# Bias with row maximum, and multiplicities with row sum, as one VectorE instruction per query tile in a ten-phase transformer kernel

## The chip, the cores and the metric

The kernel runs on one core of one Trainium2 chip. The metric is the device time of one execution in microseconds (us); three executions of the kernel before took 1783.36, 1783.44 and 1785.34 us, median 1783.44. Less is better. Shorter names used below: PE is TensorE, DVE is VectorE, ACT is ScalarE, POOL is GpSimd.

## The reference, cut to what matters

A residual stream of 256 tokens by 1024 channels, float32, passes through ten phases: two layers with a three-part mixer and a feed-forward, then two layers of feed-forward, mixer, feed-forward. Three of the attentions matter here. The differential attention of the first two mixers:

```python
dist = jnp.abs(qp[:, None] - pos[None, :]).astype(jnp.float32)
bias = -slopes[:, None, None] * dist
s1 = jnp.einsum('bqhd,bkhd->bhqk', q1b, k1).astype(jnp.float32) * scale + bias
s2 = jnp.einsum('bqhd,bkhd->bhqk', q2b, k2).astype(jnp.float32) * scale + bias
p = jax.nn.softmax(s1, axis=-1) - lam * jax.nn.softmax(s2, axis=-1)
```

It has 4 heads of width 48, each with two score matrices, and its queries and keys are RMS-normed with a gain. The banded attention of the "even" mixer (8 heads, a mask, a sink per head) is `softmax(where(valid, s, NEG_INF))` with the sink in maximum and sum. The "odd" mixer joins three dilated branches by their maxima and sums, which equals one softmax in which each key counts as many times as branches see it:

```python
wts = jnp.stack(ls) * jnp.exp(ms - jnp.max(ms, axis=0))
att = jnp.einsum('rbsh,rbshd->bshd', wts, jnp.stack(outs).astype(jnp.float32))
att = (att / jnp.sum(wts, axis=0)[..., None]).astype(h.dtype)
```

## The kernel before, in words

Every engine has its own instruction list, written out by hand, and they meet at counting semaphores. `PHASES` gives the order: mix1 0, ffn1 0, mix1 1, ffn1 1, ffn2 0, even, ffn2 1, ffn2 2, odd, ffn2 3.

All large products stream 128-column units of weights. SP loads a unit into a ring of 4 (`raw`), ACT makes its high part (`wh`, L525), DVE its low part (`wl`, L804), PE multiplies (L1210 to L1212 for the input projections of the mixers, L1223 to L1227 elsewhere). The instruction that splits unit i+4 stands in DVE's list behind the one that takes unit i out of PSUM (`y`, L1095).

In a mixer the table `W` says behind which unit of the input projection each further step stands, in the same order for every engine. Step `("attn", t)` does at once: on PE the transposition of the probabilities of head t-3 (L1327), the scores of head t (L1316) and the output of head t-4 (L1344 or L1351); on DVE `row_max` of head t and `normalise` of head t-1; on ACT the copy of the transposed probabilities (L597) and the exponentials of head t (L567). One "row" r is one 256x256 score matrix: 128 partitions by 2 query tiles of 256 keys, so 512 elements a partition. A plain head has one row, a differential head has two.

`row_max` (from L952) on a head with a bias writes `tab * bias + scores` to `pr` (L963), takes the maximum per query tile (L966) and scales it (L971). The 6 plain heads of a mix1 phase have no bias and take the maximum from PSUM. `normalise` (from L973) for the odd mixer multiplies the exponentials with the multiplicities (L981) and sums them (L982); elsewhere the sum comes out of ACT's exponential. Then come the reciprocal (L985) and the scaling (L998, or L987 to L995 for differential heads). The helper `link` puts a wait for the instruction just issued behind it: DVE goes on only when it is complete. An instruction without `link` lets the next one follow at once.

In the differential heads `tab` holds the distance |q-k| and `bias` is minus the slope times the square root of 48; in the even and odd mixers `tab` holds the mask and `bias` is 1. `head_norm` (L862) applies gain and inverse root to queries and keys. `start_values` (from L823) runs once, behind unit 8 of the first mixer, and makes small constants.

Step `post` (mix1) and `ln` (even) close a mixer, then PE starts the output projection, whose operand `mx` needs all heads.

Of the kernel before, what the change touches and what calls it, by code (L numbers as in the profile page):

```python
# [13 lines left out]
SEQ = 256  # L14
# [2 lines left out]
KD = FC // 2  # L17
RING = 4
EPS = 1e-6


PHASES = [("mix1", 0), ("ffn1", 0), ("mix1", 1), ("ffn1", 1), ("ffn2", 0), ("even", 0),
# [76 lines left out]
def build_program(nc, xin, wa, wb, prm_d, row_d, const_d, bias_d, mask_d, pw_d, out):  # L99
# [21 lines left out]
    with ctx:  # L121
        def sb(name, shape, dt=f32, c=ctx):
            return c.enter_context(nc.sbuf_tensor(name, shape, dt))
# [15 lines left out]
        tab = sb("tab", [P, 1024])  # L139
# [8 lines left out]
        eps = sb("eps", [P, 1])  # L148
        par = sb("par", [P, 32])
        small = sb("small", [P, 96])  # L150

        with ExitStack() as turn:
            gux = sb("gux", [P, 2, FC * SEQ], r32, turn)
# [29 lines left out]
        def yc(c, n=1):  # L183
            return y[:, c * SEQ:(c + n) * SEQ]
# [12 lines left out]
        def col(name, n=0):  # L197
            return prm[:, PRM[name] + n:PRM[name] + n + 1]
# [587 lines left out]
        def _(dve):  # L786
# [37 lines left out]
            def start_values():  # L824

                dve.wait_ge(s_prm, 16)
                dve.wait_ge(s_con, 48)
                dve.wait_ge(s_one, 16)
                nc.vector.tensor_copy(msk[:, :, :].rearrange("p a b -> p (a b)"), prf[:, 0:NL * P])
                l0, l1 = prm[:, PRM["lb"]:PRM["lb"] + 2], prm[:, PRM["lb"] + 2:PRM["lb"] + 4]  # L830
                link(nc.vector.tensor_tensor(par[:, 16:18], l0, l1, ALU.max))
                nc.vector.tensor_tensor(par[:, 0:2], l0, par[:, 16:18], ALU.subtract)
                nc.vector.tensor_tensor(par[:, 2:4], l1, par[:, 16:18], ALU.subtract)
                prod = qqf[:, 0:192].rearrange("p (a b) -> p a b", a=4)
                link(nc.vector.tensor_tensor(prod, view(row[:, 0:1], [[96, 4], [1, 48]]),
                                             view(row[:, 48:49], [[96, 4], [1, 48]]), ALU.mult))
                nc.vector.reduce_sum(par[:, 4:8], prod, axis=AX.X).then_inc(s_ini, 1)
                dve.wait_ge(s_inie, 1)
                link(nc.vector.tensor_tensor(par[:, 16:18], par[:, 8:10], par[:, 10:12], ALU.add))
                link(nc.vector.reciprocal(par[:, 18:20], par[:, 16:18]))  # L840
                nc.vector.tensor_tensor(par[:, 0:2], par[:, 8:10], par[:, 18:20], ALU.mult)
                link(nc.vector.tensor_tensor(par[:, 2:4], par[:, 10:12], par[:, 18:20], ALU.mult))

                link(nc.vector.tensor_tensor(par[:, 4:6], par[:, 0:2], par[:, 2:4], ALU.add))
                link(nc.vector.tensor_tensor(par[:, 20:22], par[:, 0:2], par[:, 0:2], ALU.subtract))
                link(nc.vector.tensor_tensor(par[:, 22:24], par[:, 4:6], par[:, 0:2], ALU.subtract))
                link(nc.vector.tensor_scalar(par[:, 20:24], par[:, 20:24], 0.0, None, ALU.max))
                link(nc.vector.tensor_scalar(par[:, 24:28], par[:, 20:24], -1.0, 1.0, ALU.mult, ALU.add))
                for l in range(2):
                    lam0 = 0.8 - 0.6 * math.exp(-0.3 * l)  # L850
                    link(nc.vector.tensor_tensor(par[:, 28 + l:29 + l], par[:, 13 + 2 * l:14 + 2 * l],
                                                 par[:, 12 + 2 * l:13 + 2 * l], ALU.subtract))
                    link(nc.vector.tensor_scalar(par[:, 28 + l:29 + l], par[:, 28 + l:29 + l], lam0, None, ALU.subtract))
# [4 lines left out]
            def head_norm(m, g, kind, l):  # L858
                c, gains, _ = qk_groups(kind, l)[g]
                dve.wait_ge(m["qk_rsd"], g + 1)  # L860
                for k, (name, at0) in enumerate(gains):
                    ins = nc.vector.scalar_tensor_tensor(out=yc(c + k), in0=yc(c + k), scalar=col(name, at0),  # L862
                                                         in1=sq[:, k * SEQ:(k + 1) * SEQ], op0=ALU.mult, op1=ALU.mult)
                ins.then_inc(m["qk_normed"], 1)

# [87 lines left out]
            def row_max(m, hs, t):  # L953
                h = hs[t]
                for k in range(len(h.rows)):
# [4 lines left out]
                    if h.bias is not None:  # L960
                        if r >= 6:
                            dve.wait_ge(m["probs_turned"], row_owner(hs, r - 6) + 1)
                        link(nc.vector.scalar_tensor_tensor(out=pr[:, r % 6, :], in0=tab[:, 0:512], scalar=h.bias,  # L963
                                                            in1=s, op0=ALU.mult, op1=ALU.add))
                        s = pr[:, r % 6, :]
                    link(nc.vector.reduce_max(small[:, 16 + o:18 + o], pair(s), axis=AX.X))  # L966
                    if h.sink is not None:
                        link(nc.vector.tensor_scalar(small[:, 16 + o:18 + o], small[:, 16 + o:18 + o], scale,
                                                     row[:, ROW_SINK + h.sink:ROW_SINK + h.sink + 1], ALU.mult, ALU.max))
# [3 lines left out]
            def normalise(m, hs, t, l):  # L973
# [4 lines left out]
                dve.wait_ge(m["exps"], r + nr)  # L978
                if h.cnt is not None:

                    link(nc.vector.tensor_tensor(pr[:, r % 6, :], pr[:, r % 6, :], tab[:, 512:1024], ALU.mult))  # L981
                    link(nc.vector.reduce_sum(sums, pair(pr[:, r % 6, :]), axis=AX.X))  # L982
                if h.sink is not None:
                    link(nc.vector.tensor_tensor(sums, sums, small[:, 24 + o:26 + o], ALU.add))
                link(nc.vector.reciprocal(small[:, 80 + o:80 + o + 2 * nr], sums))  # L985
# [620 lines left out]
```

## Time and profile before

| what | value |
|---|---|
| median of 3 runs | 1783.44 us |
| the profiled execution's own time | 1782.92 us |
| its span in the trace | 1781.1 us |
| PE busy | 1680.6 us (94%) |
| DVE busy | 1243.1 us (70%), 1956 instructions |
| ACT busy | 944.6 us (53%) |
| POOL busy | 512.1 us (29%) |

Span and own time differ by 1.8 us. A timeline row gives start, duration and engine, then line, operation, written tile <- read tiles, shapes and how many instructions it joins; in square brackets stands how long the engine had been idle before it and who ended that. On DVE a duration may overlap the next instruction by some 0.08 us, so the cost of an instruction in a queue is the distance between two starts.

### The profile page before, as it was taken

The numbers are of one execution on the slowest core, as the hardware profiler recorded it, in microseconds if no ns is written. First come the engines' busy times: TensorE is split into PE (matmuls) and PEld (weight loads), VectorE is DVE, ScalarE is ACT, GpSimd is POOL, SyncE is SP. The second block draws the span as 40 slices with busy tenths as digits, with TensorE's granted clock in tenths as the row PEclk, the third lists the DMA queues.
The fourth block names the chain that finished last, engine by engine and source line by source line (L and its number), as shares of the span: only waits on it lengthen the run. The fifth ranks groups of instructions, "written<-read, shape, count | busy, mean of one in ns | idle before, by whom it ended". The sixth has DMA issues, their size and how long they took to land. (4 is left out here: it accounts for less than half of the span.)

```text
span 1781.1 us, 30420 instructions
## 1 busy us (share of the span) xinstructions
PE 1680.6 (94%) x10326; PEld 1464.6 (82%) x10326; DVE 1243.1 (70%) x1956; ACT 944.6 (53%) x1550; POOL 512.1 (29%) x492
## 2 busy tenths in 40 slices
PE   7896999999987999999999978999999999799999
PEld 6784899988866999888888847888888889578887
DVE  5776777757786777667766867776577766867764
ACT  5444566544553666466646545665466534356652
POOL 0040433310213334134420004443144311444430
PEclk9998999999998999999999989999999999899999
DMA  6330355644312556555654303656465654236563
GB/s 248 106 108 24 120 188 183 219 162 152 106 59 71 166 188 203 187 172 183 208 197 132 117 1 119 187 188 209 159 188 187 209 181 154 72 108 191 186 216 101
DMA packets 71065, 274.13 MB, mean 154 GB/s; under 512 B 7888, under 2 KB 9040, under 8 KB 70992
## 3 DMA queue, kind: packets, MB, share of 16 engines
q1 hardware_dynamic: 70992, 273.17, 47.5%
q8 instruction: 44, 0.72, 0.2%
q14 instruction: 29, 0.24, 0.0%
HBM read 272.09 MB, written 1.05 MB: 153 GB/s over the span
## 5 line engine op out<-in xcount | busy, mean ns | idle before, releaser
L804 DVE TENSOR_TENSOR wl<-raw,wh 128x1024 fp32r<-128x1024 f32 (+1 forms) x474 | 624.3, 1317 | 127.6 <-ACT wh L525 121.1
L525 ACT ACTIVATE wh<-raw 128x1024 fp32r<-128x1024 f32 (+1 forms) x474 | 529.9, 1118 | 228.3 <-PE gb L1227 126.5
L1223 PE MATMUL gb<-hx,wh 128*128 128x512 f32 x1540 | 553.6, 398 | 0.0
L1224 PE MATMUL gb<-hx,wl 128*128 128x256 f32 x1540 | 432.2, 281 | 0.0
L1223 PE MATMUL gb<-gux,wh 128*128 128x512 f32 x960 | 341.3, 394 | 0.0
L1223 PEld LDWEIGHTS gb<-hx,wh 128*128 128x128 f32 x1540 | 289.8, 188 | 60.5
L1210 PE MATMUL gb<-hx,wh 128*128 128x256 f32 x1008 | 299.9, 298 | 17.7 <-DVE hx L821 9.6
L1224 PEld LDWEIGHTS gb<-hx,wl 128*128 128x128 f32 x1540 | 291.0, 189 | 7.9
L1211 PE MATMUL gb<-hx,wh 128*128 128x256 f32 x1008 | 288.9, 287 | 0.0
L1212 PE MATMUL gb<-hx,wl 128*128 128x256 f32 x1008 | 288.5, 286 | 0.0
L1224 PE MATMUL gb<-gux,wl 128*128 128x256 f32 x960 | 268.2, 279 | 0.0
L511 POOL TENSOR_TENSOR tap<-tap,rstd 128x256 f32<-128x256 f32 x132 | 175.5, 1329 | 246.0 <-ACT tap L724 139.3
L1210 PEld LDWEIGHTS gb<-hx,wh 128*128 128x128 f32 x1008 | 196.0, 194 | 30.2 <-issue 18.3
L1223 PEld LDWEIGHTS gb<-gux,wh 128*128 128x128 f32 x960 | 180.0, 188 | 39.0
L1211 PEld LDWEIGHTS gb<-hx,wh 128*128 128x128 f32 x1008 | 196.5, 195 | 5.2 <-issue 2.7
L514 POOL TENSOR_TENSOR gux<-gu,gux 128x256 f32 x132 | 142.9, 1083 | 198.9 <-ACT gux L733 198.9
L1212 PEld LDWEIGHTS gb<-hx,wl 128*128 128x128 f32 x1008 | 196.2, 195 | 0.0
L1224 PEld LDWEIGHTS gb<-gux,wl 128*128 128x128 f32 x960 | 180.4, 188 | 4.3
L430 POOL TENSOR_TENSOR sq<-x 128x256 f32<-128x256 f32 x63 | 65.0, 1031 | 241.8 <-DVE x L1170 223.2
L542 ACT ACTIVATE hx<-x,prm 128x256 fp32r<-128x256 f32 (+1 forms) x80 | 40.1, 508 | 147.1 <-DVE x L1170 143.0
L1223 PE MATMUL gb<-mx,wh 128*128 128x512 f32 x224 | 86.0, 420 | 11.4 <-DVE mx L951 7.8
L730 ACT ACTIVATE ptb<-gb 128x256 f32<-128x256 f32 x132 | 50.1, 379 | 85.0 <-PE gb L1227 85.0
(211 smaller groups left out, 2074.9 us busy)
## 6 DMA issues: line engine op xcount, KB each, us to landing
raw<-in_wa SPq DMA_DIRECT2D x378, 512.0 KB, 3.5
raw<-in_wb SPq DMA_DIRECT2D x96, 704.0 KB, 4.2
x<-in_x SPq DMA_DIRECT2D x2, 512.0 KB, 6.2
out_x<-x SPq DMA_DIRECT2D x8, 128.0 KB, 3.0
row<-in_row SPq DMA_DIRECT2D x1, 836.0 KB, 11.1
tab<-in_bias SPq DMA_DIRECT2D x3, 256.0 KB, 4.5
con<-in_const SPq DMA_DIRECT2D x1, 544.0 KB, 9.1
tab<-in_bias SPq DMA_DIRECT2D x1, 512.0 KB, 5.4
```

What stands on the lines that cost most here:

```text
L430: link(nc.gpsimd.tensor_tensor(sq[:, 0:SEQ], xc, xc, ALU.mult))
L511: nc.gpsimd.tensor_tensor(tap[:, j, :], tap[:, j, :], rstd[:, :], ALU.mult).then_inc(s_up, 1)
L514: nc.gpsimd.tensor_tensor(gul[:, part], gu[:, j, :], guh[:, part].bitcast(f32), ALU.subtract).then_inc(s_gul, 1)
L525: nc.scalar.activation(wh[:, slot, 0:nt * P], raw[:, slot, 0:nt * P], ACT.Copy).then_inc(s_hi, 1)
L542: nc.scalar.activation(hh[:, part], x[:, part], ACT.Copy, scale=prm[:, at0]).then_inc(s_hh, 1)
L730: nc.scalar.activation(low[:, j, 1, :], gb[2 * j + 1][:, SEQ:2 * SEQ], ACT.Copy).then_inc(s_vl, 1)
L804: nc.vector.tensor_tensor(wl[:, slot, 0:nt * P], raw[:, slot, 0:nt * P], wh[:, slot, 0:nt * P].bitcast(f32), ALU.subtract).then_inc(s_lo, 1)
L1210: nc.tensor.matmul(bank, a, rhs_h(k), start=start and k == 0, stop=False)
L1211: nc.tensor.matmul(bank, a, rhs_l(k), start=False, stop=False)
L1212: last = nc.tensor.matmul(bank, b, rhs_h(k), start=False, stop=stop and k == nt - 1)
L1223: nc.tensor.matmul(bank[:, :], a, both(k), start=start and k == 0, stop=False)
L1224: nc.tensor.matmul(bank[:, 0:SEQ], b, high(k), start=False, stop=False)
```

## The change

`row_max` on a head with a bias issues one `tensor_tensor_reduce` per query tile in place of L963 and L966: `pr = (tab + scores) * bias`, with the maximum of that row as a second result. `normalise` in the odd mixer issues one per query tile in place of L981 and L982. Only the second of each two is followed by `link`. For `(tab + s) * bias` to be the old `tab * bias + s`, the queries of the differential heads are divided by `bias`, through eight more gain columns `bqs` that `start_values` computes.

```diff
+LOWEST = -3.0e38
...
+        bqs = small[:, 88:96]
...
                 for l in range(2):
+                    for h in heads("mix1"):
+                        if h.bias is not None:
+                            nc.vector.tensor_scalar(bqs[:, 4 * l + h.h:4 * l + h.h + 1], col("bq", l), 1.0 / h.bias, None, ALU.mult)
...
-                    ins = nc.vector.scalar_tensor_tensor(out=yc(c + k), in0=yc(c + k), scalar=col(name, at0),
+                    gain = col(name, at0) if name != "bq" else bqs[:, 4 * l + (c - M1_B) // 2:4 * l + (c - M1_B) // 2 + 1]
+                    ins = nc.vector.scalar_tensor_tensor(out=yc(c + k), in0=yc(c + k), scalar=gain,
                                                          in1=sq[:, k * SEQ:(k + 1) * SEQ], op0=ALU.mult, op1=ALU.mult)
...
-                        link(nc.vector.scalar_tensor_tensor(out=pr[:, r % 6, :], in0=tab[:, 0:512], scalar=h.bias,
-                                                            in1=s, op0=ALU.mult, op1=ALU.add))
-                        s = pr[:, r % 6, :]
-                    link(nc.vector.reduce_max(small[:, 16 + o:18 + o], pair(s), axis=AX.X))
+                        for qt in range(2):
+                            cs = slice(qt * SEQ, (qt + 1) * SEQ)
+                            last = nc.vector.tensor_tensor_reduce(out=pr[:, r % 6, cs], in0=tab[:, cs], in1=s[:, cs], scale=h.bias,
+                                                                  scalar=LOWEST, op0=ALU.add, op1=ALU.max,
+                                                                  accum_out=small[:, 16 + o + qt:17 + o + qt])
+                        link(last)
+                    else:
+                        link(nc.vector.reduce_max(small[:, 16 + o:18 + o], pair(s), axis=AX.X))
...
-                    link(nc.vector.tensor_tensor(pr[:, r % 6, :], pr[:, r % 6, :], tab[:, 512:1024], ALU.mult))
-                    link(nc.vector.reduce_sum(sums, pair(pr[:, r % 6, :]), axis=AX.X))
+                    for qt in range(2):
+                        p1 = pr[:, r % 6, qt * SEQ:(qt + 1) * SEQ]
+                        last = nc.vector.tensor_tensor_reduce(out=p1, in0=p1, in1=tab[:, 512 + qt * SEQ:512 + (qt + 1) * SEQ], scale=1.0,
+                                                              scalar=0.0, op0=ALU.mult, op1=ALU.add,
+                                                              accum_out=sums[:, qt:qt + 1])
+                    link(last)
```

The lists of PE, ACT, POOL and SP stay as they were. On DVE, one head of the odd mixer before (`row_max` of a head, `normalise` of the head before it, then the next unit):

```order
L963 SCALAR_TENSOR_TENSOR pr<-tab,mb 128x512
L966 TENSOR_REDUCE small<-pr 128x2
L971 TENSOR_SCALAR small<-small 128x2
L981 TENSOR_TENSOR pr<-pr,tab 128x512
L982 TENSOR_REDUCE small<-pr 128x2
L985 RECIPROCAL small<-small 128x2
L998 TENSOR_SCALAR pr<-pr,small 128x256 x2
L1095 TENSOR_TENSOR y<-gb,rstd 128x256
L804 TENSOR_TENSOR wl<-raw,wh 128x1024
```

The same place in the changed kernel, whose line numbers are shifted (L981, L999, L1012, L1109 and L806 are the old L971, L985, L998, L1095 and L804):

```order
L971 ISA pr,small<-tab,mb 128x256
L971 ISA small 128x1
L971 ISA pr,small<-tab,mb 128x256
L971 ISA small 128x1
L981 TENSOR_SCALAR small<-small 128x2
L993 ISA pr,small<-pr,tab 128x256
L993 ISA small 128x1
L993 ISA pr,small<-pr,tab 128x256
L993 ISA small 128x1
L999 RECIPROCAL small<-small 128x2
L1012 TENSOR_SCALAR pr<-pr,small 128x256 x2
L1109 TENSOR_TENSOR y<-gb,rstd 128x256
```

Each `tensor_tensor_reduce` is two instructions: the work on 256 elements, and one that writes the reduced value of one element. Two instructions have become four in each of the 32 biased rows and 8 multiplicity rows. The second place is `start_values` on DVE, in the changed kernel:

```order
L849 TENSOR_SCALAR par<-par 128x4
L850 TENSOR_SCALAR par<-par 128x4
L854 TENSOR_SCALAR small<-prm 128x1 x4
L856 TENSOR_TENSOR par<-par 128x1
L858 TENSOR_SCALAR par<-par 128x1
L854 TENSOR_SCALAR small<-prm 128x1 x4
L856 TENSOR_TENSOR par<-par 128x1
```

The two groups of four at L854 are new; nothing is linked to them.

## Rows read from the trace of the kernel before

**Rows 1.** The page: busy us (share of the span) x instructions of each engine.
```profile
PE 1680.6 (94%) x10326; PEld 1464.6 (82%) x10326; DVE 1243.1 (70%) x1956; ACT 944.6 (53%) x1550; POOL 512.1 (29%) x492
```

**Rows 2.** Groups of DVE instructions by form: count, busy us, mean ns, idle before.
```profile
L963 DVE SCALAR_TENSOR_TENSOR pr<-tab,mb 128x512 f32<-128x512 f32 x32 | 21.9, 685 | 8.7 <-PE mb L1316 8.7
L981 DVE TENSOR_TENSOR pr<-pr,tab 128x512 f32<-128x512 f32 x8 | 6.0, 754 | 0.0
L995 DVE SCALAR_TENSOR_TENSOR pr<-pr,small 128x256 f32<-128x256 f32 x16 | 7.0, 481 | 0.3
```

**Rows 3.** Timeline of DVE, one head of the odd mixer.
```profile
1509.92 0.17 DVE L971 TENSOR_SCALAR small<-small 128x2 f32<-128x2 f32 x1
1510.00 0.68 DVE L981 TENSOR_TENSOR pr<-pr,tab 128x512 f32<-128x512 f32 x1
...
1511.44 0.17 DVE L985 RECIPROCAL small<-small 128x2 f32<-128x2 f32 x1
1511.64 0.62 DVE L998 TENSOR_SCALAR pr<-pr,small 128x256 f32<-128x256 f32 x2
1512.17 0.42 DVE L1095 TENSOR_TENSOR y<-gb,rstd 128x256 f32<-128x256 f32 x1
1512.51 1.22 DVE L804 TENSOR_TENSOR wl<-raw,wh 128x1024 fp32r<-128x1024 f32 x1
```

**Rows 4.** Timeline of ACT, even mixer: exponentials that also give a row sum.
```profile
1042.87 0.51 ACT L567 ACTIVATE pr<-pr,small 128x256 f32<-128x256 f32 x1 [2.37 <-DVE small L971]
1043.28 0.19 ACT L567 ACTIVATION_READ_ACCUMULATOR pr<-pr,small 128x1 f32 x1
1043.38 0.49 ACT L567 ACTIVATE pr<-pr,small 128x256 f32<-128x256 f32 x1
```

**Rows 5.** Timeline of DVE, two 512-element instructions with no wait between.
```profile
39.84 0.68 DVE L871 TENSOR_TENSOR ptb<-mb,con 128x512 f32<-128x512 f32 x1
40.44 0.68 DVE L872 TENSOR_TENSOR y<-y,con 128x512 f32<-128x512 f32 x1
```

**Rows 6.** Timelines at the end of mixer mix1 0, DVE and PE.
```profile
148.79 0.88 DVE L862 SCALAR_TENSOR_TENSOR y<-y,prm,sq 128x256 f32<-128x256 f32 x2 [1.65 <-ACT sq L620]
...
160.46 1.78 PE L1344 MATMUL mb<-tv,ptb 128*128 128x96 f32 x7 [4.58 <-DVE mx L1029]
```

**Rows 7.** Timeline of PE, even mixer: two waits.
```profile
1025.01 0.48 PE L1360 MATMUL mb<-sq,con 128*128 128x256 f32 x1 [2.03 <-POOL sq L444]
...
1052.24 0.40 PE L1351 MATMUL mb<-ptb,tv 128*64 128x256 f32 x1 [2.59 <-ACT ptb L597]
```

**Rows 8.** The chain that ended last, in order of time: start us, us, what.
```profile
1018.77 0.61 DVE pr L963
...
1047.94 0.70 DVE pr L963
...
1503.90 0.61 DVE pr L963
...
1550.14 0.60 DVE pr L981
```

**Rows 9.** Timeline of PE, odd mixer: three waits.
```profile
1523.79 0.63 PE L1327 MATMUL mb<-con,pr 128*128 128x128 f32 x4 [2.05 <-ACT sq L618]
...
1546.47 0.63 PE L1327 MATMUL mb<-con,pr 128*128 128x128 f32 x4 [1.84 <-DVE mx L1086]
...
1553.98 1.09 PE L1327 MATMUL mb<-con,pr 128*128 128x128 f32 x4 [3.24 <-DVE mx L1086]
```

**Rows 10.** Windows of odd: PE, PEld, DVE, ACT, POOL busy, granted clock, DMA share, GB/s.
```profile
1519.00:1525.00 6.00, 2.57 (x10) 1.33 (x10) 5.83 (x12) 3.60 (x6) 2.82 (x4) 0.98 0.27 87
1525.00:1534.00 9.00, 9.00 (x39) 6.67 (x37) 5.29 (x12) 2.21 (x5) 3.03 (x7) 0.64 0.17 58
```

**Rows 11.** Timelines of DVE and PE, mix1 0, behind unit 8.
```profile
60.04 1.23 DVE L804 TENSOR_TENSOR wl<-raw,wh 128x1024 fp32r<-128x1024 f32 x1 [1.71 <-ACT wh L525]
...
85.20 0.58 PE L1210 MATMUL gb<-hx,wh 128*128 128x256 f32 x1 [5.09 <-DVE y L1095]
```

## The prediction

> **What bounds the kernel now.** First the page: PE is busy for 94% of the span and DVE for 70% [rows 1], so a faster DVE helps only where PE stands idle for it. Such places are the ends of the mixers and most of the odd mixer, so I read the waits of PE there, then DVE's timeline in the same stretches, then the chain that ended last. The chain covers the part from 1001 us on; for the two mix1 phases I followed the timelines.
>
> What the change touches are pairs of two 512-element instructions, each followed by a wait for its completion: L963 with L966 (32 times), L981 with L982 (8 times, 754 ns in the mean against 685, because single ones run beside POOL) [rows 2]. In the queue a pair takes from 1510.00 to 1511.44, that is 1.44 us [rows 3].
>
> **The new pair.** It is work on 256 elements, read-out, work on 256 elements, read-out, and a wait only behind the last. No row shows such an instruction, so I price it by its nearest neighbours. Two-input work on 256 elements, with no wait behind it, holds the queue from 1512.17 to 1512.51, 0.34 us. A tiny instruction without a wait holds it from 1509.92 to 1510.00, 0.08 us, and one with a wait from 1511.44 to 1511.64, 0.20 us [rows 3]. The sum is 0.34 + 0.08 + 0.34 + 0.20 = 0.96 us, a saving of 0.48 us a pair. That is the low end, too: no piece has a cheaper neighbour. That the parts overlap like this is what ACT does with its own row sums: the read-out is recorded at 0.19 us but holds the queue for 0.10 (1043.28 to 1043.38), and the main instruction before it holds it for 0.41 of its 0.51 [rows 4]. The high end: the reduction takes two cycles an element, so each half costs what 512 elements cost, and every part runs to its end before the next starts: twice (0.72 + 0.20) = 1.84 us, with half of today's 1.44 for one of 512 elements, 0.40 dearer than today. I take 0.96, since rows 3 and rows 4 both show the queue moving on before an instruction ends.
>
> **Which pairs lie on the path.** A pair counts where DVE's end is what PE finally waits for.
>
> - mix1, twice: the heads of the differential attention are DVE's at the very end. In mix1 0 DVE last waits for ACT at 148.79; from there it works without a pause through the rows of the last two heads, 4 pairs, to the instruction for which PE waits 4.58 us at 160.46 [rows 6]. The pairs of the first two such heads are hidden: PE's last projection unit and the products of the scan (L1394) cover them. With that cover gone they would still be behind POOL's squares. mix1 1 repeats the pattern. So 2 x 4 pairs, 8 x 0.48 = 3.8 us.
> - even: 8 pairs, of which the chain holds 3, from 1018.77 to 1047.94 [rows 8]. The first ends in PE's wait for POOL at 1025.01 (2.03 us); the others, one head before the last but one and the last, end in PE's waits up to the one of 2.59 us at 1052.24 [rows 7]. Between the first and the second PE's convolution products bound, and pairs vanish beneath them. 3 x 0.48 = 1.4 us.
> - odd: 16 pairs, 12 in the chain, from L963 at 1503.90 to L981 at 1550.14 [rows 8]. Six come before PE's wait of 2.05 us at 1523.79, four before the 1.84 us at 1546.47, two before the 3.24 us at 1553.98 [rows 9]. The first six ask for 2.9 us, more than that wait; but PE stood idle for 6 - 2.57 = 3.4 us between 1519 and 1525 [rows 10], the rest of it for POOL's squares, which follow a late L1095 of DVE. So there is room. 12 x 0.48 = 5.8 us.
>
> Together 23 pairs, 11.0 us. What is late next is PE itself, or ACT in the heads' exponentials, which move with the maxima.
>
> **What it adds.** Eight tiny instructions in `start_values`, 8 x 0.08 = 0.64 us. They look hidden in 1780 us and are not: they stand ahead of unit 8's L1095 and of a row maximum; ACT's exponentials and with them its next weight split follow that maximum, DVE waits for the split (1.71 us at 60.04), and this goes round until PE waits 5.09 us for DVE at 85.20 [rows 11]. So +0.6 us. The gain column of `head_norm` only comes from another tile, same form: nothing. The longer exposure of `small` costs nothing.
>
> **The clock.** In the odd mixer PE was busy for only 2.57 us of the 6 us from 1519 to 1525, and then worked through 9 us at a granted clock of 0.64, at 1.2 instead of 2.4 GHz for most of it [rows 10]. In that stretch PE is the bound, so the low clock costs (1 - 0.64) x 9 = 3.2 us. The change takes 2.9 us out of just this idle time. If most of the gap closes, the clock need not fall, and 3.2 us come back; DVE's own work there (two more pairs, shorter by 1 us) would just keep up. I count it in. Elsewhere the idle gaps of PE stay long (4.58 us at 160.46 becomes 2.7) and I take the clock as unchanged, plus or minus 1.5 us.
>
> **Sum.** -11.0 + 0.6 - 3.2 = -13.6 us against the profiled execution's 1782.92 us: 1769.3. The median of the runs stands 0.5 us above it, so I forecast 1769.8 us. A measurement of this kernel can tell about 0.2%, 3.6 us, from no change.
>
> **A rule that speaks against it.** The 16 instructions at L995, a scalar-tensor-tensor with both inputs in SBUF, took 481 ns for 256 elements [rows 2], and L1095 with one input in PSUM 0.42 us [rows 3]: two SBUF streams alone don't halve the rate here, which would be near the 685 ns of 512 elements. But neither has a reduced output. The Trainium skill, Vector Engine (DVE) Microarchitecture Reference, section "Points that are easy to get wrong", warns that a scalar-tensor-tensor with two SBUF sources that are not bf16 runs at half throughput, since no read port is left for the accumulator. By that rule the multiplicity pairs (both inputs in SBUF) would be slow and the bias pairs (scores in PSUM) not. No run here shows it.
>
> **The rivals.**
>
> 1. As forecast, but the clock falls all the same: 1769.8 + 3.2 = 1773.0 us. For it: other gaps of PE remain and a fall needs no large one; against it: the gap was 60% of six microseconds and is now nearly filled. Chance 0.27.
> 2. Reduction from two SBUF streams at half rate (the mechanism of the rule above). 512 elements with no wait hold the queue for 0.60 us [rows 5], so such a pair is 0.60 + 0.08 + 0.60 + 0.20 = 1.48 us, 0.52 more than forecast. Five of the 12 in the odd chain are of this kind: 2.6 us back, which also lets the gap at 1523 stand, 3.2 more at worst: 1772.4 to 1775.6. Chance 0.10.
> 3. Each read-out waits for the end of its main instruction, and the next for it: 0.45 + 0.20 + 0.45 + 0.20 = 1.30 us, with the 0.42 us of L1095 and the 0.03 us between the end of L985 and the next start [rows 3]. The saving is 0.14 x 23 = 3.2 us, less 0.6, and the clock stays low: 1783.4 - 2.6 = 1780.8 us, no change that can be told. Against it: rows 4. Chance 0.08.
> 4. The other side: two cycles an element in every reducing instruction, and no overlap, so 1.84 us a pair. 23 x 0.40 + 0.6 = 9.8 us: 1793.2 us. It decides from a pair of 1.41 us on (slower by more than 0.2% from 1.57). For it: four instructions replace two, of a kind that this program never ran. Against: ACT's reducing form is no slower than its plain one. Chance 0.05.
>
> The forecast has 0.45; 0.05 is left for what I don't see, such as the new instructions meeting POOL's as L981 did in its mean of 754 ns [rows 2].
>
> **Range and chances.** From 1765.5 (the clock also holds in one mixer's end) to 1777.5, which takes in rivals 1 and 2. Left out are rivals 3 and 4 and tails, under 0.2. Faster by over 0.2% (below 1779.9): forecast, rivals 1 and 2 and part of the rest, 0.86. Within 0.2%: rival 3, 0.08. Slower: 0.06.
>
> **What would show it.** In the new profile the two mains of a pair start 0.42 us apart, and the pair takes 0.96 us to the next start (rival 3: 1.30; rivals 2 and 4: 0.68 or more between the starts). PE's wait at the end of mix1 0 falls from 4.58 to about 2.7 us; the stretch from mix1's unit 8 to PE's wait at 85.20 is 0.6 us longer; the odd mixer from its first L963 to the output projection is 9 us shorter, with a granted clock near 1 where rows 10 have 0.64. Wrong would be a pair over 1.3 us, or a pair at 0.96 with the odd mixer shorter by less than 4 us.

## The result and the profile after

The changed kernel takes 1764.47 us (median of 4 runs, 1763.29 to 1764.66), the kernel before, on the same chip, 1783.4 us (4 runs, 1779.64 to 1785.34). The ratio is 0.9897, with an interval from 0.9882 to 0.9913. So the gain is 18.9 us, where 13.6 were forecast: the direction was right, and the time lies 1 us below the low end of the range, 1765.5.

| | before | after |
|---|---|---|
| median, us | 1783.4 | 1764.47 |
| span of the profiled execution, us | 1781.1 | 1762.7 |
| mean granted clock of TensorE | 0.971 | 0.978 |
| DVE busy, us | 1243.1 | 1221.2 |
| PE's wait at the end of mix1 0, us | 4.58 | 3.33 |
| PE's waits in odd, us: first / second / third | 2.05 / 1.84 / 3.24 | 1.02 / 0 / 4.32 |

The page of after, the line of busy times (before: [rows 1]):

```profile
PE 1669.1 (95%) x10326; PEld 1459.4 (83%) x10326; DVE 1221.2 (69%) x2044; ACT 943.8 (54%) x1550; POOL 511.0 (29%) x492
```

DVE has 88 instructions more and 22 us less busy time. PE is busy 11.5 us less for the same 10326 matmuls. The kernel has not taken work from PE, so those 11.5 us already point at the clock.

The groups of DVE's instructions after, by form: count, busy us, mean ns, idle before (before: [rows 2]):

```profile
L971 DVE CUSTOM_DVE_ANT_0 pr<-tab,mb 128x256 f32<-128x256 f32 x64 | 24.3, 416 | 9.9 <-PE mb L1330 9.9
L993 DVE CUSTOM_DVE_ANT_0 pr<-pr,tab 128x256 f32<-128x256 f32 x16 | 7.9, 531 | 0.0
L971 DVE DVE_READ_ACCUMULATOR2_ANT small<- 128x1 f32 x64 | 5.2, 82 | 0.0
L993 DVE DVE_READ_ACCUMULATOR2_ANT small<- 128x1 f32 x16 | 1.2, 77 | 0.0
```

And the timeline of DVE after, in one head of the odd mixer (before: [rows 3]):

```profile
1499.48 0.41 DVE L971 CUSTOM_DVE_ANT_0 pr<-tab,mb 128x256 f32<-128x256 f32 x1
1499.82 0.08 DVE L971 DVE_READ_ACCUMULATOR2_ANT small<- 128x1 f32 x1
1499.82 0.41 DVE L971 CUSTOM_DVE_ANT_0 pr<-tab,mb 128x256 f32<-128x256 f32 x1
1500.16 0.08 DVE L971 DVE_READ_ACCUMULATOR2_ANT small<- 128x1 f32 x1
1500.27 0.17 DVE L981 TENSOR_SCALAR small<-small 128x2 f32<-128x2 f32 x1
1500.35 0.42 DVE L993 CUSTOM_DVE_ANT_0 pr<-pr,tab 128x256 f32<-128x256 f32 x1
1500.69 0.08 DVE L993 DVE_READ_ACCUMULATOR2_ANT small<- 128x1 f32 x1
1500.69 0.42 DVE L993 CUSTOM_DVE_ANT_0 pr<-pr,tab 128x256 f32<-128x256 f32 x1
1501.04 0.08 DVE L993 DVE_READ_ACCUMULATOR2_ANT small<- 128x1 f32 x1
1501.15 0.17 DVE L999 RECIPROCAL small<-small 128x2 f32<-128x2 f32 x1
```

The reader is to compare the starts, not the durations. From 1499.48 to 1500.27 the pair holds the queue for 0.79 us: 0.34 + 0.34 + 0.11. A read-out starts at the same moment as the next main instruction, at 1499.82, so it takes no room of its own; and the wait behind the last one costs 0.11 us. The prediction had 0.96, with 0.08 and 0.20 for these two. The saving is 1.44 - 0.79 = 0.65 us a pair instead of 0.48.

**Where the time went.** PE issues the same matmuls in the same order in every kernel of this study, so its k-th matmul is the same work in all of them, and the difference of its starts is a running account. The table takes six marks, the matmuls that start nearest to 130, 200, 600, 1000, 1100 and 1480 us of before, and 1600 us as the last, and gives by how many us each stretch between them is shorter (-) or longer (+) than in the profile of before. The 400 us from 600 to 1000, the 380 us from 1100 to 1480 and all that follows 1600 move by 0.2 us at most in any kernel, and stand together as "rest".

| kernel | start, to 130 | end of mix1 0, to 200 | ffn and mix1 1, to 600 | even, 1000 to 1100 | odd, 1480 to 1600 | rest | span |
|---|---|---|---|---|---|---|---|
| forecast | +0.6 | -1.9 | -1.9 | -1.4 | -9.0 | 0 | -13.6 |
| the change | -0.31 | -3.56 | -1.03 | -3.83 | -9.66 | +0.03 | -18.37 |

The chain of reasons is in PE's waits. The timeline of PE after, at the end of mix1 0 (before: the wait of 4.58 us at 160.46, [rows 6]):

```profile
157.67 1.10 PE L1358 MATMUL mb<-tv,ptb 128*128 128x96 f32 x8 [3.33 <-DVE mx L1043]
```

The same for the even mixer (before: [rows 7]):

```profile
1019.47 0.70 PE L1374 MATMUL mb<-sq,con 128*128 128x256 f32 x2 [1.40 <-POOL sq L446]
1037.39 1.05 PE L1365 MATMUL mb<-ptb,tv 128*64 128x256 f32 x4 [0.99 <-DVE mx L1043]
1043.78 1.05 PE L1365 MATMUL mb<-ptb,tv 128*64 128x256 f32 x4 [2.10 <-ACT ptb L599]
1047.44 1.39 PE L1365 MATMUL mb<-ptb,tv 128*64 128x256 f32 x8 [0.44 <-DVE mx L1043]
```

And for the odd mixer (before: 1523.79, 1546.47 and 1553.98, [rows 9]):

```profile
1512.43 0.63 PE L1341 MATMUL mb<-con,pr 128*128 128x128 f32 x4 [1.02 <-ACT sq L620]
...
1529.70 0.63 PE L1341 MATMUL mb<-con,pr 128*128 128x128 f32 x4
...
1537.35 0.67 PE L1341 MATMUL mb<-con,pr 128*128 128x128 f32 x4 [4.32 <-DVE mx L1100]
```

In odd the first wait is halved, the second is gone, and the third has grown from 3.24 to 4.32 us, since PE now comes to it earlier. The windows of odd after, with the columns of [rows 10] (window, its length, busy us of PE, PEld, DVE, ACT and POOL, granted clock, DMA share, GB/s):

```profile
1508.00:1514.00 6.00, 4.98 (x32) 3.68 (x30) 5.44 (x17) 3.77 (x6) 3.89 (x7) 1.00 0.28 90
1514.00:1520.00 6.00, 6.00 (x39) 4.78 (x39) 3.83 (x15) 2.45 (x4) 2.41 (x5) 1.00 0.26 85
1520.00:1526.00 6.00, 6.00 (x40) 4.63 (x38) 5.84 (x16) 2.72 (x5) 3.97 (x5) 1.00 0.27 87
```

Where PE had stood idle for 3.4 of 6 us it is now idle for 1.0, and behind it the granted clock is 1.00, 2.4 GHz, where it had been 0.64 for nine microseconds.

### The profile page after: what moved, and what is told of

Read it like the earlier page. It is cut to its first block and busy times, and to the rows that moved or that the text cites. A ratio compares the mean times of both kernels' runs of the same rounds, so it can differ in the third digit from the quotient of the medians.

```text
span 1762.7 us, 30508 instructions
## 1 busy us (share of the span) xinstructions
PE 1669.1 (95%) x10326; PEld 1459.4 (83%) x10326; DVE 1221.2 (69%) x2044; ACT 943.8 (54%) x1550; POOL 511.0 (29%) x492
## 3 DMA queue, kind: packets, MB, share of 16 engines
HBM read 272.09 MB, written 1.05 MB: 155 GB/s over the span
## 5 line engine op out<-in xcount | busy, mean ns | idle before, releaser
L806 DVE TENSOR_TENSOR wl<-raw,wh 128x1024 fp32r<-128x1024 f32 (+1 forms) x474 | 624.7, 1318 | 129.0 <-ACT wh L527 122.8
```

The lines of the kernel that those rows point to most:

```text
L806: nc.vector.tensor_tensor(wl[:, slot, 0:nt * P], raw[:, slot, 0:nt * P], wh[:, slot, 0:nt * P].bitcast(f32), ALU.subtract).then_inc(s_lo, 1)
```

## The experiments

Twelve runs follow, of eleven kernels: the kernel with a wait behind both instructions ran twice, and one of the eleven is the change itself, again. Every time stands against runs of the kernel before on the same chip; the phase stretches are each profile's own. First the two halves of the change.

### Bias pairs alone

```diff
-                    for qt in range(2):
-                        p1 = pr[:, r % 6, qt * SEQ:(qt + 1) * SEQ]
-                        last = nc.vector.tensor_tensor_reduce(out=p1, in0=p1, in1=tab[:, 512 + qt * SEQ:512 + (qt + 1) * SEQ], scale=1.0,
...
-                    link(last)
+                    link(nc.vector.tensor_tensor(pr[:, r % 6, :], pr[:, r % 6, :], tab[:, 512:1024], ALU.mult))
+                    link(nc.vector.reduce_sum(sums, pair(pr[:, r % 6, :]), axis=AX.X))
```

> Only the bias pairs are fused (32 rows); the multiplicity pairs of the odd mixer stay as two 512-element instructions. 18 of the 23 path pairs are of this kind. Theory A (a fused pair costs 0.79 us, the read-outs take no room of their own, each saves 0.65): 18 x 0.65 - 0.6 = 11.1 us under the kernel before, 1772.3; and if the 2.6 us that the first four pairs of the odd mixer take from PE's idle time are enough to keep the clock up there, another 3.2 less: 1769.1. Theory B (a fused pair saves the forecast 0.48 and the rest of the gain came from the clock alone): 8.0 us without the clock, 1775.4.

Measured: 1764.63 us (1763.46 to 1766.16) against 1781.07, ratio 0.991 [0.9894, 0.9927], so 16.4 us. The even mixer is 3.91 us shorter, as with the whole change, and the odd one 8.98 of the 9.66. The bias pairs carry nearly all of the gain. Theory A had 14.3 us with the high clock, theory B 8.0; the result is above both and nearest to A.

### Multiplicity pairs alone

The edit is the other half: the bias pairs and the query gains as before, no work added in `start_values`.

> Only the 8 multiplicity pairs are fused; bias and maximum, the query gains and start_values are those of before. Five path pairs, two of them ahead of the idle time at 1523. Theory A: 5 x 0.65 = 3.3 us, and the clock still falls in the odd mixer because 2 us of idle time remain: 1780.2. If the clock holds all the same: 1777.0. The rule of half rate for two float32 inputs from SBUF with a reduction: no gain, 1783.4 or a little over.

Measured: 1777.3 us (1776.1 to 1779.76, 10 runs) against 1781.07, ratio 0.9981 [0.9971, 0.999], so 3.8 us, near theory A's 3.3. All eight pairs are in the odd mixer, which is 2.80 us shorter and runs 17.1 us at the half clock where before runs 20.5. DVE's timeline of this kernel, whose L983 is the fused instruction with both inputs in SBUF:

```profile
1506.54 0.42 DVE L983 CUSTOM_DVE_ANT_0 pr<-pr,tab 128x256 f32<-128x256 f32 x1
1506.88 0.08 DVE L983 DVE_READ_ACCUMULATOR2_ANT small<- 128x1 f32 x1
1506.88 0.42 DVE L983 CUSTOM_DVE_ANT_0 pr<-pr,tab 128x256 f32<-128x256 f32 x1
```

It takes 0.42 us and 0.34 of the queue, as L971 of after does with one input in PSUM. Rival 2 is refuted for this instruction. The Trainium skill, Vector Engine (DVE) Microarchitecture Reference, section "Points that are easy to get wrong", has a scalar-tensor-tensor with two SBUF sources that are not bf16 at half throughput; this fused multiplication and row sum, in float32 from two SBUF tiles, doesn't run so.

In the odd mixer the two halves give 8.98 + 2.80 = 11.8 us apart and 9.66 together. Part of it is the gap, which can be closed only once: the matmul at 1523.79 us of before comes 2.21 us earlier with the bias pairs, 0.87 with the multiplicity pairs and 2.68 with both. That is 0.4 of the 2.1 us. The rest arises behind it, and no run takes it apart. It is not time at the half clock counted twice: the halves remove 13.7 and 3.4 us of that, and the whole change removes 17.1.

### A wait behind both instructions of each pair

```diff
-                        link(last)
+                            link(last)
```

The `link`, a wait for completion, moves into the loop over the two query tiles; the same at the multiplicities. This kernel ran twice. The first time:

> The changed kernel with a wait for completion behind both instructions of a pair instead of behind the second alone. Theory A (the first read-out is hidden under the second main instruction): each half costs 0.45 us, a pair 0.90 instead of 0.79, 23 x 0.11 = 2.5 us more than the changed kernel, 1767.0. Rival (the read-out is free however it stands, the time is the main instruction's alone): under 1 us more.

Measured: 1764.35 us (1763.31 to 1765.9), ratio 0.9906 [0.9889, 0.9922]. DVE's timeline of this run:

```profile
1499.92 0.41 DVE L971 CUSTOM_DVE_ANT_0 pr<-tab,mb 128x256 f32<-128x256 f32 x1
1500.26 0.08 DVE L971 DVE_READ_ACCUMULATOR2_ANT small<- 128x1 f32 x1
1500.37 0.42 DVE L971 CUSTOM_DVE_ANT_0 pr<-tab,mb 128x256 f32<-128x256 f32 x1
1500.71 0.08 DVE L971 DVE_READ_ACCUMULATOR2_ANT small<- 128x1 f32 x1
1500.83 0.17 DVE L981 TENSOR_SCALAR small<-small 128x2 f32<-128x2 f32 x1
```

The pair takes 0.91 us, 0.12 more: 0.45 us to the next start behind each main instruction. The second time it stood beside the whole change (below):

> The whole change with a wait for completion behind both instructions of every pair, beside the whole change on the same chip. The trace of the first such run showed a pair of 0.91 us against 0.79. Theory A (a pair on the path costs what its queue room costs): 23 x 0.12 = 2.8 us over the whole change, less what the multiplicity pairs beside PE-bound stretches hide, so 1.5 to 2.8. Theory B (the first such run came out level with the whole change on another chip, so the wait is absorbed: PE, not DVE, bounds by now): under 0.7 us over it.

Measured: 1764.92 us (1762.17 to 1766.54, 5 runs) against the whole change's 1762.68; ratios to before 0.9905 [0.9889, 0.9922] and 0.9892 [0.9877, 0.9908]. The 2.2 us between the medians lie within theory A's 1.5 to 2.8, but the intervals overlap, so the times don't decide. PE's account shows which pairs count. At the end of mix1 0, where four pairs are on the path, PE's mark is 0.48 us later than in the changed kernel's profile (4 x 0.12), and as much at the end of mix1 1. In even, the three pairs make it later by 0.14, 0.26 and 0.39 us, one by one. In odd the marks at 1523.79, 1546.47 and 1553.98 us of before move by 0.03 us at most. So 8 + 3 pairs still set those marks, and the twelve in odd, once they are fused, do not.

The end of the program hardly feels even the eleven. In even the 0.39 us are gone at the mark of 1100 us. From the mark at 130 us to the end, the changed kernel's two profiles take 1632.9 and 1633.2 us, and the two of this kernel 1633.6 and 1632.9. By the marks theory A is right, by the total theory B. What gives the time back behind the marks is not taken apart here.

### The idle time of the odd mixer put back

```diff
             def attention(m, kind, hs, t, l):
+                if kind == "odd" and t == 3:
+                    for _ in range(4):
+                        link(nc.vector.tensor_tensor(gu[:, :, :], gu[:, :, :], gu[:, :, :], ALU.max))
                 if t < len(hs):
                     row_max(m, hs, t)
```

The four instructions leave their tile as it is. They were to take 2.9 us of DVE and take 3.7, since the first of them, which runs beside POOL, takes 1.53 us and the others 0.69:

```profile
1506.55 3.71 DVE L1037 TENSOR_TENSOR gu<-gu 128x512 f32<-128x512 f32 x4
1510.29 0.42 DVE L971 CUSTOM_DVE_ANT_0 pr<-tab,mb 128x256 f32<-128x256 f32 x1
```

> The changed kernel with four linked 512-element VectorE instructions on an unused buffer (0.72 us each, 2.9 us) ahead of the row maximum of head 3 in the odd mixer, which gives TensorE its idle time near the end of that head's step back. Theory of the clock: the granted clock falls to 1.2 GHz again for some 6 us behind it, as it did before, and the time rises by 2.9 + 3.2 = 6.1 us over the changed kernel, to 1770.6. Rival (the fall has nothing to do with this idle time): 2.9 us, 1767.4, and no stretch at half the clock there.

Measured: 1771.17 us (1769.92 to 1772.04), ratio 0.9946 [0.9929, 0.9963], 6.5 and 6.8 us above the two kernels that ran beside it with the bias pairs and without such idle time (1764.63 and 1764.35). The windows of odd:

```profile
1508.00:1514.00 6.00, 1.66 (x9) 0.86 (x8) 5.70 (x18) 2.67 (x5) 0.81 (x3) 0.85 0.20 77
1514.00:1520.00 6.00, 6.00 (x17) 3.69 (x18) 4.09 (x15) 1.90 (x4) 2.89 (x5) 0.50 0.27 87
1520.00:1526.00 6.00, 6.00 (x34) 4.90 (x32) 1.73 (x2) 1.54 (x2) 1.80 (x3) 0.80 0.00 0
```

With PE busy for only 1.66 of 6 us, the next six run at 0.50, at 1.2 GHz, on 17 matmuls where the whole change has 39. By PE's account the instructions make it 3.3 us later at once, and the low clock 3.9 us more by 1540 us of before. By the end of the mixer it is 7.3 us behind the changed kernel. That is the prediction's mechanism, in its direction and its size: idle time at this place costs about twice what it lasts.

### The whole change again, and the gains on POOL

> The whole change again, unchanged, as the measure for the three kernels that run beside it. 1764.5 us, as before, if the chip is like the others; the sum of the two part gains measured apart (16.4 for the bias pairs with the start values, 3.8 for the multiplicity pairs) would be 20.2 us. Theory A (the parts partly buy the same thing, the high clock of the odd mixer, which either needs only once, and from the first six pairs of the odd mixer PE becomes the bound): the whole gains 0.5 to 3 us less than that sum, 17.2 to 19.7. Theory B (the parts are independent): 20.2 us, within 0.5.

Measured: 1762.68 us (1762.22 to 1764.76, 5 runs) against 1781.7 (15 runs), ratio 0.9892 [0.9877, 0.9908], so 19.0 us against 20.2 for the halves. That is within A, but the intervals are too wide to separate A from B by the times; the odd mixer's stretches above do.

```diff
+            pool.wait_ge(s_prm, 16)
+            for l in range(2):
+                for h in heads("mix1"):
+                    if h.bias is not None:
+                        last = nc.gpsimd.tensor_scalar(bqs[:, 4 * l + h.h:4 * l + h.h + 1], col("bq", l), 1.0 / h.bias, None, ALU.mult)
+            link(last)
```

(ahead of POOL's first phase, and gone from `start_values`).

> The whole change, but the eight tiny inverse-slope gains are computed by POOL before its first phase instead of by DVE in start_values. Theory A (they stand on DVE's path at the start and cost 0.47 us there, as the marks of PE show by 68.8 us): 0.4 to 0.6 us under the whole change of the same chip, PE's mark at 68.8 us earlier by that, and no other difference. Theory B (they are hidden, and the 0.47 us came from something else): no difference. Rival on the other side: POOL's own first work shifts by the eight instructions, at most 1 us later, and PE waits for it: same or up to 0.5 us slower.

Measured: 1764.32 us (1760.37 to 1764.83, 5 runs), ratio 0.9901 [0.9886, 0.9917]: no difference that the times can tell from the whole change. PE's account between 55 and 89 us of before shows one: in the whole change, and also in the kernel with mix1 alone, the matmul at 68.77 us loses 0.48 us against before; with the gains on POOL it loses 0.00, and so it does in the kernel without gains (odd alone, below). So the added work costs 0.48 us where the prediction had 0.6, and it sits where the prediction put it. Taking it away is right in the profile and too small to be confirmed in the time; I don't call this version faster.

### One mixer at a time

Three kernels fuse the pairs in one kind of mixer and leave the others as before. Mix1 alone keeps the query gains and their start values; odd alone and even alone have neither. The edit of the kernel before, for odd (the multiplicities in the same way):

```diff
-                        link(nc.vector.scalar_tensor_tensor(out=pr[:, r % 6, :], in0=tab[:, 0:512], scalar=h.bias,
-                                                            in1=s, op0=ALU.mult, op1=ALU.add))
-                        s = pr[:, r % 6, :]
-                    link(nc.vector.reduce_max(small[:, 16 + o:18 + o], pair(s), axis=AX.X))
+                        if kind == "odd":
+                            for qt in range(2):
...
+                            link(last)
+                        else:
+                            link(nc.vector.scalar_tensor_tensor(out=pr[:, r % 6, :], in0=tab[:, 0:512], scalar=h.bias,
+                                                                in1=s, op0=ALU.mult, op1=ALU.add))
+                            link(nc.vector.reduce_max(small[:, 16 + o:18 + o], pair(pr[:, r % 6, :]), axis=AX.X))
```

> Fused bias pairs in the two mix1 phases alone; even, odd and the multiplicities as before the change, the start values kept. Theory A (8 pairs on the path at 0.65 us each, 0.5 us of start values, clock unchanged but for 0.5 to 1 us at the end of mix1 0): 4.7 to 5.7 us under before, so about 1776. Theory B (pairs worth the 0.48 us of the prediction, no clock): 3.3 us. Theory C (the 3 us by which the clock outran the forecast comes from mix1's ends): 7.5 us or more. In the trace the half-clock stretch of the odd mixer must be there again, about 6.8 us long.

> Both kinds of pair fused in the odd mixer alone, everything else as before the change (no start values). Theory A (the odd mixer gives 5.1 us by its pairs and 4.6 by the clock, and neither depends on the other phases): 9 to 10.5 us under before, the stretch at 1525 to 1534 us at the high clock and the mixer's last stretch shorter at the low clock. Theory B (the high clock in the odd mixer needs the state that the earlier phases leave): 5 to 6.5 us, the half-clock stretch stands. Theory C (the pairs are worth more here than the marks of PE say): over 11 us.

> Bias pairs fused in the even mixer alone. Theory A (3 pairs on the path and some clock at the mixer's end): 2.0 us by the pairs and 0 to 2 us by the clock, so 2 to 4 us under before. Theory B (the prediction's sizes): 1.4 us and no clock. Theory C (the clock of the even mixer's end goes the other way round without the changed phases ahead): 0 to 1 us, or slower. With the mix1 phases alone (3.1 us measured, 4.7 to 5.7 expected) and the odd mixer alone the three sum to the whole's 19 us if the phases are independent: 3.1 + 9.7 + 3 is 15.8, so one of them should then be larger than A says.

Measured: mix1 alone 1778.58 us (10 runs), ratio 0.9984 [0.9974, 0.9994], 3.1 us, nearest theory B's 3.3; odd alone 1772.38 us (4 runs), ratio 0.9948 [0.9932, 0.9965], 8.4 us by the medians, a little under A's 9 to 10.5; even alone 1780.07 us (10 runs), ratio 0.9998 [0.9988, 1.0007], nothing that can be told, theory C. For mix1 alone B has the number but not the reason: its profile has the four pairs at the end of mix1 0 at 2.48 us, 0.62 each, as the whole change has, and loses time elsewhere (below). The three ratios leave 0.70% together (0.16 + 0.02 + 0.52), the whole change has 1.08%. So the parts don't add up: 0.38% are missing, about 7 us, more than the four intervals together explain if their errors are independent (0.27%). The stretches of the profiles say where, and how many us PE ran at the half clock in even and odd (worked out as twice the stretch times one minus its mean granted clock):

| kernel | start | end of mix1 0 | to 600 | even | odd | half clock in even | half clock in odd |
|---|---|---|---|---|---|---|---|
| before | 0 | 0 | 0 | 0 | 0 | 20.5 | 20.5 |
| the change | -0.31 | -3.56 | -1.03 | -3.83 | -9.66 | 17.1 | 3.4 |
| the change, again | -0.34 | -3.39 | -0.92 | -3.97 | -9.66 | 17.1 | 3.4 |
| bias pairs alone | -1.67 | -3.77 | -1.14 | -3.91 | -8.98 | 17.1 | 6.8 |
| multiplicity pairs alone | -2.26 | -0.14 | -0.44 | -0.66 | -2.80 | 20.5 | 17.1 |
| idle time put back | -2.28 | -2.55 | -1.83 | -3.87 | -2.37 | 17.1 | 13.7 |
| a wait behind both, first | -0.33 | -3.21 | -0.96 | -3.82 | -9.50 | 17.1 | 3.4 |
| a wait behind both, second | -2.64 | -3.39 | -1.31 | -3.84 | -9.61 | 17.1 | 3.4 |
| gains on POOL | -3.47 | -3.93 | -1.85 | -3.83 | -9.61 | 17.1 | 3.4 |
| mix1 alone | -2.70 | -3.74 | -1.16 | -0.49 | +0.98 | 20.5 | 20.5 |
| odd alone | -2.53 | +0.15 | -0.05 | 0.00 | -7.38 | 20.5 | 10.2 |
| even alone | -2.38 | -0.04 | -0.02 | -1.00 | +0.95 | 23.9 | 20.5 |

Three things are to be seen. First, a stretch in which nothing was fused stays as it was within 0.7 us, but for odd, which is 1 us longer in two kernels that leave it alone. With it mix1 alone adds up roughly: -3.74 - 1.16 in its own stretches, -0.49 in even, +0.98 in odd and +0.5 for the gains are -3.9, where the medians have 3.1 us. Second, even and odd gain more in the whole change than when fused alone, 3.83 against 1.00 and 9.66 against 7.38. Up to the matmul at 1546.47 us of before, odd alone is as much earlier as the whole change, 8.11 and 8.10 us; what it lacks comes behind the last wait, where it runs 10.2 us at the half clock and the whole change 3.4. Third, the start differs by some 2.5 us between kernels whose start is the same: the profile of before runs 3.4 us at the half clock at 26 us, those of odd, even and mix1 alone run none there. This is a draw between executions: of the two profiles of one kernel, the one with a wait behind both, the first has it and the second hasn't, -0.33 and -2.64 us.

The even mixer shows the second most plainly. PE's timeline in the kernel with even alone:

```profile
1021.97 0.70 PE L1378 MATMUL mb<-sq,con 128*128 128x256 f32 x2 [1.40 <-POOL sq L445]
1041.57 1.05 PE L1369 MATMUL mb<-ptb,tv 128*64 128x256 f32 x4 [0.99 <-DVE mx L1047]
1047.96 1.94 PE L1369 MATMUL mb<-ptb,tv 128*64 128x256 f32 x4 [2.11 <-ACT ptb L598]
1053.14 1.39 PE L1369 MATMUL mb<-ptb,tv 128*64 128x256 f32 x8 [0.44 <-DVE mx L1047]
```

The waits are those of the whole change to a hundredth: 1.40, 0.99, 2.11 and 0.44 us. But between the first and the second row lie 19.60 us against 17.92, and between the third and the fourth 5.18 against 3.66, and the four matmuls at 1047.96 take 1.94 us against 1.05. It is the same work at half the clock, 3.2 us in sum.

### The start made later

Does the moment decide at which a mixer is reached? In the whole change even is reached 5 us earlier than before.

```diff
                 link(nc.vector.tensor_scalar(par[:, 24:28], par[:, 20:24], -1.0, 1.0, ALU.mult, ALU.add))
+                for _ in range(24):
+                    link(nc.vector.tensor_scalar(par[:, 20:24], par[:, 20:24], 1.0, None, ALU.mult))
```

and the same with 12.

> The whole change, with 24 linked tiny instructions (0.20 us each) added in start_values: everything after the start runs about 4.8 us later, and nothing else differs. Question: in the profiles the even mixer (marks of PE at 1000 and 1100 us of before) became 3.8 to 4.0 us shorter in the whole change, but only 1.0 us in the kernel that fuses the even mixer alone, with the same instructions in it; and half-clock time in it was 17.1 us against 23.9. Theory A (when a mixer's gaps come relative to something outside the program decides which stretches run at the half clock; an earlier start of 5 to 6 us shifted them): with the start 4.8 us later the even mixer gains 1 to 2 us instead of 3.8, and the ends of mix1 change by 1 us or more too. Theory B (the earlier phases' own shape, not the moment, leaves another clock behind): even stays at -3.8, odd at -9.6, mix1 0 at -3.5, each within 0.3. The whole is 4.8 us slower than the whole change by B; by A 5 to 9 us.

> The same with 12 of them, 2.4 us later. Theory A: the phases' own times move again, at least one mixer by 1 us or more, not necessarily halfway. Theory B: all phases as in the whole change within 0.3, the whole 2.4 us slower.

Measured: 1767.28 us (1765.13 to 1769.6), ratio 0.9915 [0.9898, 0.9931], with 24; 1765.39 us in a single run with 12. With 24 that is 15.1 us under before, 3.8 less than the change gives, where B had 4.8 less. In the profiles the start is longer by 3.9 us than in the change with 24 and by 1.0 with 12, where the draw of the start's clock fell otherwise. The rest stands still: mix1 0 -3.65 and -3.73, to 600 -1.17 and -1.00, even -3.89 and -3.87, odd -9.71 and -9.69. Theory A falls and B stands, for shifts of this size: a later start does nothing, the mixers keep what they have.

The moment is excluded only as counted from the start of the program. The trace's records of the granted clock show the two shifted kernels in the same place against the clock's own changes. From the last rise of the clock in mix1 1 to the matmul at 1000 us of before, 440.28 us pass in the change, 440.35 with 24 instructions and 440.40 with 12, but 441.18 in even alone and 441.20 before. And in even the clock falls once in the change, at 1053.12 us for 17.07 us, but three times in even alone, at 1023.94, 1047.83 and 1058.07 us. That the fused ends of mix1 move the mixer by 0.9 us against the clock's changes, and that this decides which of its gaps are followed by the half clock, is a rival that fits these numbers. No run moves that distance by itself, so what the earlier phases hand on stays open.

## Why the prediction was off by five microseconds

The account of the change, 18.4 us of span, splits into what the pairs give at the marks where PE waits and what is left, the clock:

| term | forecast | measured |
|---|---|---|
| pairs, end of mix1 0 | -1.9 | -2.5 |
| pairs, mix1 1 | -1.9 | -2.5 |
| pairs, even | -1.4 | -1.9 |
| pairs, odd | -5.8 | -4.6 |
| start | +0.6 | -0.3 (+0.5 for the gains; -0.6 ahead of 57 us and -0.2 behind 89, not of the change) |
| clock, odd | -3.2 | -5.1 |
| clock, elsewhere | 0 | -1.5 |
| sum | -13.6 | -18.4 |

The pair terms are the shifts at the marks of 160.46, 534.09 (both 2.5 us from their stretch's start), 1025.01, 1045.20 and 1052.24 (0.65 + 0.63 + 0.65), and in odd 1523.79 (2.7) and 1546.47 (1.9). The clock is the rest of each stretch, so it also holds small things that I don't name: -5.1 in odd, -1.9 in even, -1.1 and +1.5 in the two of mix1.

- **The new pair** was priced 0.17 us too dear: 0.79 us, not 0.96. The failing items are the read-out, 0.08 for which the queue gives nothing, and the wait at the end, 0.11 instead of 0.20. "That is the low end, too: no piece has a cheaper neighbour" was wrong. Rows 4, which the same paragraph quoted, had a read-out recorded at 0.19 and holding the queue for 0.10; that an overlap could go all the way I should have kept as the low end. This step was mis-sized. Rivals 2, 3 and 4, with their pairs of 1.48, 1.30 and 1.84 us, fell.
- **The count of pairs on the path** was right for mix1 and even (4 + 4 + 3, and the kernel with a wait behind both instructions shows them at PE's marks) and wrong in odd. The first six were to give 2.9 us at 0.48, and give 2.7 at 0.65, since PE bounds in between: DVE now stands still for PE there, 0.83 us at 1496.93. The last two give nothing that the account shows. Twelve pairs at 0.65 would be 7.8 us; 4.6 came. So a pair priced too dear and a list too long nearly cancelled, by luck: 11.0 forecast, 11.5 measured.
- **The clock in odd** was right as a mechanism and at its place: the 9 us at 0.64 are at 1.00 now, worth the 3.2 us, and the idle time put back brings the low clock back. Rival 1, the clock falling all the same, did not come. The prediction's stretch ended at 1534, however, and the clock also rose in the mixer's last stretch, which it had not looked at.
- **"Elsewhere ... I take the clock as unchanged, plus or minus 1.5 us"** is the step that failed. Behind the prediction's 9 us the clock gave 3.4 us: about 1.9 in odd's tail and 1.9 in even, less 0.4 that it took in the two of mix1. That is beyond the 1.5 us that the step allowed. The half-clock time fell from 20.5 to 17.1 in even and from 20.5 to 3.4 in odd. The range allowed one such stretch ("the clock also holds in one mixer's end"), and there were two, with a cheaper pair on top. That is why it missed by 1 us.
- **The start**: 0.48 us for the eight instructions where 0.6 was said; right.
- **The wait at the end of mix1 0** was to fall from 4.58 to 2.7 us and is 3.33: PE itself comes 1.2 us earlier to it, for the maxima that it waits for on the way are earlier as well. A wait that shrinks by less than the path did is no sign that the path didn't shrink.

Of the five us, then, 0.5 is in the pairs, 0.9 at the start (mostly no effect of the change), and 3.4 in the clock.

## What to carry to other kernels

Price an instruction by the distance to the next start, for its read-out and its wait too, and let "it overlaps entirely" be the low end of its price. Where PE stands idle for a good part of a stretch at full clock, give what closes the gap its own clock term, and look for such a term in every mixer and not only in the largest; here the clock gave more than a third of the gain by the split above. Where one part is measured alone, look at the stretches of its profile and not only at its time: the same even mixer gave 1.0 us alone and 3.8 in company.

## What the runs showed that I had not expected

- A row reduction's read-out (73 to 84 ns in the changed kernel) takes no room in DVE's queue if the next instruction doesn't wait for it: two main instructions start 0.34 us apart with or without it between them. With a wait the distance is 0.45 us.
- Beside POOL the fused multiplication stretches. The timeline of DVE after, and under it POOL's for the same stretch:

```profile
1533.63 0.41 DVE L993 CUSTOM_DVE_ANT_0 pr<-pr,tab 128x256 f32<-128x256 f32 x1
1533.97 0.08 DVE L993 DVE_READ_ACCUMULATOR2_ANT small<- 128x1 f32 x1
1533.97 0.94 DVE L993 CUSTOM_DVE_ANT_0 pr<-pr,tab 128x256 f32<-128x256 f32 x1
```

```profile
1533.08 0.61 POOL L484 TENSOR_TENSOR kk<-qq 128x256 f32<-128x256 f32 x1
1533.77 0.85 POOL L484 TENSOR_TENSOR qq<-kk 128x256 f32<-128x256 f32 x1
```

  Of two equal instructions, one takes 0.41 us and the next, begun while POOL works from SBUF to SBUF, 0.94. Four of the 16 are stretched, to 0.82 to 0.95 us, and all four lie beside such work of POOL; two others, at 0.41 us, have it beside them for 0.3 us. L971, with its scores in PSUM, has a mean of 416 ns over 64, and the 16 of them that lie beside POOL take 404 to 421. That POOL is the cause is read off these coincidences; no run takes its work away. In the kernel with a wait behind both, the stretched one takes 0.82 us and its pair ends no later: the stretch takes up the wait. That this is why the odd mixer no longer feels 0.12 us a pair is a reading of these rows, not shown by a run of its own.
- The same instructions with the same waits ran 17.1 or 23.9 us at the half clock in the even mixer, depending on what the phases some hundred microseconds ahead were made of; within one program the stretches behind the start repeat to 0.4 us in two pairs of profiles. Between programs with the same mix1 the one to 600 us differs by 0.9 (-1.85 with the gains on POOL, -0.92 to -1.03 in the change).
